# One activation table set behind the tanh, root inputs straight from PSUM, low parts ahead of sums, a last store in three parts

## The reference, cut to what matters

```
def rmsnorm(x, g):
    xf = x.astype(jnp.float32)
    xf = xf * lax.rsqrt(jnp.mean(xf * xf, axis=-1, keepdims=True) + RMS_EPS)
    return (xf * g.astype(jnp.float32)).astype(x.dtype)

def merge_and_mlp(h, gates, y_a, y_b, y_c, w_out, norm_mlp_g, w_up, w_down):
    mixed = gates[0] * y_a + gates[1] * y_b + gates[2] * y_c
    h = h + mixed @ w_out
    hn = rmsnorm(h, norm_mlp_g)
    return h + jnp.square(jax.nn.relu(hn @ w_up)) @ w_down

y_prompt = rmsnorm(h_p, norm_final_g)
y_sample = rmsnorm(h_s, norm_final_g)
```

## Time and profile before

| | before |
|---|---|
| median of 3 runs | 1104.13 us (1103.65 to 1106.02) |
| profiled execution, its own time | 1104.08 us |
| its span, first to last instruction | 1102.3 us |
| PE busy | 1050.9 us (95%) |
| DVE, ACT, POOL busy | 453.5, 422.0, 310.7 us |
| mean granted PE clock | 0.986 of full |

### The profile page before, as it was taken

The page is one execution under the profiler, slowest core; times in us unless marked ns, Lnnn a source line. Parts: engine busy times, 40 slices in busy tenths (PEclk is TensorE's granted clock), DMA queues, the critical chain, the costliest instruction groups (busy, mean ns, idle before and its releaser), DMA issues.

```text
span 1102.3 us, 21957 instructions
## 1 busy us (share of the span) xinstructions
PE 1050.9 (95%) x8694; PEld 947.8 (86%) x8694; DVE 453.5 (41%) x805; ACT 422.0 (38%) x730; POOL 310.7 (28%) x141
## 2 busy tenths in 40 slices
PE   6999999998999989999999999989999999999995
PEld 6886778876778667778999999989999999999995
DVE  5313455775145523333543476743113212212434
ACT  5214556674233222334333323454134224313534
POOL 2422232211222220001212122224443444334620
PEclk9999999999999998999999999999999999999998
DMA  7588887774885575511422325736557367467202
GB/s 270 181 271 300 288 249 232 262 238 153 291 279 197 174 267 178 187 58 40 174 96 88 100 82 190 283 111 248 207 203 272 137 243 284 145 258 267 77 1 78
DMA packets 65945, 211.08 MB, mean 191 GB/s; under 512 B 7850, under 2 KB 10155, under 8 KB 63667
## 3 DMA queue, kind: packets, MB, share of 16 engines
q1 hardware_dynamic: 65842, 209.67, 55.2%
HBM read 202.16 MB, written 51.48 MB: 230 GB/s over the span
## 4 chain that ended last, share of the span: by engine, by line
PE 83%; DVE 5%; ACT 4%; issue 3%; DMA 2%; SPq 1%; POOL 1%; DVEq 0%; ACTq 0%
PE G L1284 52%; PE S L1284 14%; PE Z L1284 11%; PE TR L1287 3%; PE OU L1284 2%; DMA wraw<-in_w_in_dram 2%; ACT whi L681 1%; POOL wlo L653 1%; DVE convy L958 1%; SPq L543 1%; SPq L544 1%; ACT lg L824 0%; DVE mtmp L958 0%; DVE macc L955 0%; DVE pw L1149 0%
## 5 line engine op out<-in xcount | busy, mean ns | idle before, releaser
L1284 PE MATMUL G<-xh,whi 128*128 128x260 f32 x1288 | 380.3, 295 | 14.2 <-DVE xl L958 9.8
L1284 PE MATMUL G<-xl,whi 128*128 128x260 f32 x1288 | 366.8, 285 | 0.0
L1284 PE MATMUL G<-xh,wlo 128*128 128x260 f32 x1288 | 366.1, 284 | 0.0
L653 POOL TENSOR_TENSOR wlo<-wraw,whi 128x1024 fp32r<-128x1024 f32 x61 | 149.1, 2444 | 533.1 <-ACT whi L681 533.1
L1284 PEld LDWEIGHTS G<-xh,whi 128*128 128x128 f32 x1288 | 246.0, 191 | 44.2 <-issue 29.5
L1284 PEld LDWEIGHTS G<-xl,whi 128*128 128x128 f32 x1288 | 245.9, 191 | 0.0
L1284 PEld LDWEIGHTS G<-xh,wlo 128*128 128x128 f32 x1288 | 245.4, 191 | 0.0
L653 POOL TENSOR_TENSOR wlo<-mraw,whi 128x1024 fp32r<-128x1024 f32 x56 | 135.2, 2415 | 201.6 <-ACT whi L681 201.5
L681 ACT ACTIVATE whi<-wraw 128x1024 fp32r<-128x1024 f32 x83 | 87.9, 1059 | 221.8 <-PE G L1284 185.1
L681 ACT ACTIVATE whi<-mraw 128x1024 fp32r<-128x1024 f32 x56 | 59.4, 1061 | 157.3 <-PE G L1284 54.9
L955 DVE TENSOR_TENSOR tg<-G,rstd 128x260 f32<-128x260 f32 x48 | 20.4, 427 | 85.1 <-PE G L1284 85.0
(11 more groups left out here) (261 smaller groups left out, 2090.3 us busy)
## 6 DMA issues: line engine op xcount, KB each, us to landing
wraw<-in_w_in_dram SPq DMA_DIRECT2D x66, 512.0 KB, 5.0
kv<-in_kpool_dram SPq DMA_DIRECT2D x128, 256.0 KB, 3.3
kv<-in_vpool_dram SPq DMA_DIRECT2D x128, 256.0 KB, 3.4
mraw<-in_w_up_dram SPq DMA_DIRECT2D x32, 512.0 KB, 3.5
mraw<-in_w_down_dram SPq DMA_DIRECT2D x32, 512.0 KB, 3.5
out_win_k_kept_dram<-in_cache_win_k_dram SPq DMA_DIRECT2D x8, 2047.0 KB, 9.1
out_win_v_kept_dram<-in_cache_win_v_dram SPq DMA_DIRECT2D x8, 2047.0 KB, 10.5
wraw<-in_w_ab_dram SPq DMA_DIRECT2D x8, 512.0 KB, 3.4
```

What stands on the lines that cost most here:

```text
L653: nc.gpsimd.tensor_tensor(low(u), raw(u)[0], high(u).bitcast(F32), ALU.subtract).then_inc(w_lo, 1)
L1284: return nc.tensor.matmul(out, lhsT, rhs, start=start, stop=stop, **kw)
```

## The change

Four things change.

1. ACT loads the set that has both Ln and Exp once, right behind the last tanh. The eight loads at the second and third norm go.
2. At all three norms Ln reads the bank itself (scale 1/D, bias EPS from a new column of the constants), and DVE makes its variance only after Ln has read the bank (it waits for `xln_made`, `hln_made`, `yln_made`).
3. In the output projection's tiles ACT copies to `xh` ahead of the square, and DVE writes `xl` ahead of the sum (`h_low` ahead of `h_sum`). Besides, ACT writes the high part of the MLP's third unit (`SPLIT_AFTER[UP_TICK + 1]`) at `UP_TICK` itself, ahead of the first tick's squares.
4. At the end the eighth square of each half isn't added on DVE: PE adds it in PSUM with a second matmul. The second half's multiplications and stores come in three parts (3, 3 and 2 tiles).

```diff
+Y_PARTS = (((0, 4), (4, 4)), ((0, 3), (3, 3), (6, 2)))
...
+            def rough_root(out, total, ln_made, root_made, h):
+                nc.scalar.activation(out, total[:, 0:HALF], ACT.Ln, scale=1.0 / D, bias=eps).then_inc(ln_made, 1)
+                act.wait_ge(ln_made, h + 1)
+                nc.scalar.activation(out, out, ACT.Exp, scale=-0.5).then_inc(root_made, 1)
...
-                await_taken(act, "x_var", h)
-                nc.scalar.activation(rstd[:, half(h)], xvar[:, 0, half(h)], ACT.Ln).then_inc(xln_made, 1)
-                act.wait_ge(xln_made, h + 1)
-                nc.scalar.activation(rstd[:, half(h)], rstd[:, half(h)], ACT.Exp, scale=-0.5).then_inc(xroot_made, 1)
+                src = await_bank(act, "x_var", h)
+                rough_root(rstd[:, half(h)], src, xln_made, xroot_made, h)
...
             def h_ready_tile(t):
                 act.wait_ge(dve_took, at("out", t) + 1)
+                act.wait_ge(hn_made, t + 1)
+                copy(xh[:, t, :], hn[:, t % 2, :]).then_inc(hn_hi, 1)
                 if t:
                     act.wait_ge(hacc_made, t)
                 nc.scalar.activation(h2[:], hT[:, t, :], ACT.Square).then_inc(h2_made, 1)
-                act.wait_ge(hn_made, t + 1)
-                copy(xh[:, t, :], hn[:, t % 2, :]).then_inc(hn_hi, 1)
...
-                for v in SPLIT_AFTER.get(k, []):
-                    split_hi(v)
+                if k != UP_TICK + 1:
+                    for v in SPLIT_AFTER.get(k, []):
+                        split_hi(v)
+                if k == UP_TICK:
+                    for v in SPLIT_AFTER.get(k + 1, []):
+                        split_hi(v)
                 if job[0] in ("g0", "g1", "g2"):
                     gate(k, int(job[0][1]), tile, h)
+                    if job[0] == "g2" and tile == KC - 1 and h:
+                        nc.scalar.preload_act_table_set("natural_log_exp_and_others")
...
                 src = await_bank(dve, "x_var", h)
+                dve.wait_ge(xln_made, h + 1)
...
-                    dve.wait_ge(hsum_made, h + 1)
+                    dve.wait_ge(hln_made, h + 1)
...
             def y_sum(n):
+                if n % KC == KC - 1:
+                    return
...
+            def h_low(t):
                 dve.wait_ge(hn_hi, t + 1)
                 tt(xl[:, t, :], hn[:, t % 2, :], xh[:, t, :].bitcast(F32), ALU.subtract).then_inc(hn_lo, 1)
...
                     if tile:
+                        h_low(tile - 1)
                         h_sum(tile - 1)
                     if tile == KC - 1:
+                        h_low(tile)
                         h_sum(tile)
...
             def y_total(h):
+                out = bank[("TR", "OU")[h]][:, 0:HALF]
                 pe.wait_ge(hvar_made, h + 1)
-                pe.wait_ge(yacc_made, KC * (h + 1))
-                mm(bank[("TR", "OU")[h]][:, 0:HALF], ones[:], yacc[:, half(h)], True, True).then_inc(ysum_made, 1)
+                pe.wait_ge(yacc_made, (KC - 1) * (h + 1))
+                mm(out, ones[:], yacc[:, half(h)], True, False)
+                pe.wait_ge(ysq_made, KC * (h + 1))
+                mm(out, ones[:], ysq[:, (KC - 1) % 2], False, True).then_inc(ysum_made, 1)
```

More of the change, by code:

```diff
@@ L296 @@
 for _name, _w in (("gmix", KC), ("gmlp", KC), ("gfin", KC), ("bgate", 3 * KC), ("convw", 12), ("bsb", SBH), ("bcol", 1),
-                  ("st", 64), ("dmask", 8), ("smask", 8), ("sel4", 4), ("sel8", 8)):
+                  ("st", 64), ("dmask", 8), ("smask", 8), ("sel4", 4), ("sel8", 8), ("eps", 1)):
     CV[_name] = (_n, _w)
@@ L351, in decoder_step @@
         dmask, sel4, sel8 = vec("dmask"), vec("sel4"), vec("sel8")
-        smask = vec("smask")
+        smask, eps = vec("smask"), vec("eps")
         xraw = place("xraw", [P, KC, TOK], R + 12928)
@@ L619, in _ @@
                     sp.dma_start(o["conv_old"], x["state_conv"][0, :, 1]).then_inc(conv_copy, 16)
-            for n in range(4):
+            y_parts = [(h, t, w_) for h in range(2) for t, w_ in Y_PARTS[h]]
+            for n, (h, t, w_) in enumerate(y_parts):
                 sp.wait_ge(y_made, n + 1)
-                t = 4 * (n % 2)
-                sp.dma_start(o["y"][:, t:t + 4, half(n // 2)], yT[:, t:t + 4, half(n // 2)]).then_inc(y_out, 16)
-            sp.wait_ge(y_out, 16 * 4)
+                sp.dma_start(o["y"][:, t:t + w_, half(h)], yT[:, t:t + w_, half(h)]).then_inc(y_out, 16)
+            sp.wait_ge(y_out, 16 * len(y_parts))
             sp.wait_ge(win_out, 16 * 6 * NB)
@@ L889, in mlp_root @@
                 for h in range(2):
[L890 to L893, removed]
+                    act.wait_ge(hsum_made, h + 1)
+                    rough_root(rstdb[:, half(h)], bank[("TR", "OU")[h]], hln_made, hroot_made, h)
             def hidden(k, t, h):
@@ L906, in y_square @@
                 act.wait_ge(dve_took, k + 1)
-                if n >= 2:
-                    act.wait_ge(yacc_made, n - 1)
+                if n == KC + 1:
+                    act.wait_ge(ysum_made, 1)
+                elif n >= 2:
+                    act.wait_ge(yacc_made, n - 1 - (n - 2) // KC)
                 nc.scalar.activation(ysq[:, n % 2], hT[:, t, half(h)], ACT.Square).then_inc(ysq_made, 1)
@@ L912, in y_root @@
             def y_root(h):
[L913 to L916, removed]
+                act.wait_ge(ysum_made, h + 1)
+                rough_root(yrstd[:, half(h)], bank[("TR", "OU")[h]], yln_made, yroot_made, h)
             for k, (u, job, h, last) in enumerate(TICKS):
@@ L1111, in y_sum @@
                 else:
-                    dve.wait_ge(yacc_made, n)
+                    dve.wait_ge(yacc_made, n - n // KC)
                     tt(part, part, ysq[:, n % 2], ALU.add).then_inc(yacc_made, 1)
             def y_root(h):
-                dve.wait_ge(ysum_made, h + 1)
+                dve.wait_ge(yln_made, h + 1)
                 nc.vector.tensor_scalar(yvar[:, 0, half(h)], bank[("TR", "OU")[h]][:, 0:HALF], 1.0 / D, EPS, ALU.mult,
@@ L1120, in y_root @@
                 link(polish(yrstd[:, half(h)], yvar[:, 0, half(h)], yvar[:, 1, half(h)]))
[L1121 to L1124, removed]
+                for t, w_ in Y_PARTS[h]:
+                    dve.wait_ge(yg_made, KC * h + t + w_)
+                    part = yT[:, t:t + w_, half(h)]
+                    tt(part, part, yrstd[:, half(h)].unsqueeze(1).to_broadcast([P, w_, HALF]),
                        ALU.mult).then_inc(y_made, 1)
@@ L1646, in column_vectors @@
     put("sel4", ((r // 32)[:, None] == np.arange(4)[None, :]).astype(np.float32))
+    put("eps", EPS)
     put("sel8", ((r % 32 // 4)[:, None] == np.arange(8)[None, :]).astype(np.float32))
```

## The result

| | before | changed |
|---|---|---|
| median, first comparison | 1103.98 us (1103.30 to 1108.82, 6 runs) | 1096.47 us (1094.93 to 1098.62, 6 runs) |
| ratio of the times | | 0.9932, 95% interval 0.9908 to 0.9956 |
| all executions, mean | 1103.74 us (66) | 1097.37 us (12) |
| profiled execution, its own time | 1104.08 us | 1096.90 us |
| its span | 1102.3 us | 1095.1 us |

The change is faster, by 7.5 us in the first comparison and by 6.4 us between the means of all executions of this study (by their scatter 5.4 to 7.4 with 95%).

A forecast was written before the change was run, and what follows sets the result against it. PE was taken to bound the kernel (83% of a 1102.3 us span). Terms 0.3 - 0.35 - 2.9 + 0.44 - 2.1 = -4.6 us, from 1104.08 us, gave 1099.5 us; range 1097.6 to 1101.5.

The forecast's parts named there:

- The low parts at the last output tile: Last output tile: low parts ahead of sums let PE start its eighth block earlier; -0.35 us, bounds 0.28 and 0.62.
- the third unit's high part and the loads: MLP's fifth tick: PE's whole 2.78 us stall for POOL goes, with a restart of 0.1; -2.9 us.
- The end: Last norm and stores: +0.44 us for a second matmul between ticks, -2.1 us from a shorter chain and earlier stores.
- The new load, the other tiles: Load behind the last tanh and the other output tiles: both fit in ACT's idle time; 0 us.
- The first norm: First norm: later second variance and Newton instructions held by POOL lengthen PE's wait; +0.3 us, between +0.1 and +0.6.
- the marks that would have shown the prediction wrong: Wait at MLP's fifth tick or later, over 1.5 us at first norm, last-store gap, or low clock where it was 1.00.
- the rival on a hidden wait: At the end: a table load carries a hidden wait that goes with it, 1.38 us, giving 1098.0; chance 0.02.
- one more: Clock falls once more, or for longer, since ticks stand elsewhere in time: 1.5 us lost, 1101.0; chance 0.14.
- the clock stays up in the MLP's first ticks: MLP's first ticks: the clock no longer falls to 0.50, so 1.5 us come back, 1098.0; chance 0.15.

The follow-up runs named there:

- the kernel with both halves undone: Changed kernel with the second norm's four table loads back and the MLP third unit's high part late again; 1101.35 us, ratio 0.9977.

## Why the prediction missed

**The terms held.** *The low parts at the last output tile* and *the third unit's high part and the loads* were -0.35 and -2.9 and came to -3.27 where the clock did the same in both executions (the order by itself 0.29, between the bounds 0.28 and 0.62). *The end* was +0.44 and -2.1 and came to +0.41 and -2.10. *The new load, the other tiles* was 0: no new wait of PE shows there. *The first norm* was +0.3 and is 0.30 at its place. The sum without the first norm was -4.9, and the four stretches sum to -4.96. Of the marks that would have shown the prediction wrong, only the last one came: low clock in a window that had 1.00, at 10 to 20 us.

A load costs what the rows said. From Ln's start to the Newton step there are now 0.96 us; before it was 2.19 from the earlier trace rows, of which the load is 1.30 (Ln got 0.08 longer). No 1.38 of drain came back on top: the rival on a hidden wait falls, and with it, for this kernel, the figure of the Trainium skill, "ScalarE: Activation LUTs", section "What ACT_TABLE_LOAD costs".

**The step that failed is *The third unit's high part and the loads*, with the clock behind the stall put at nothing.** The term was the wait of 2.78 and "a restart of 0.1", since the one profile at hand showed the clock up behind that wait, and the sum was then made against that one execution. Falls were priced only as rivals, with chances of 0.14 for one more and 0.15 for one less, and the place for one less in the MLP's first ticks. The profiles show falls at five or six places, and they are drawn anew in each execution, but for those near 375 and 413, which all fourteen profiles have. Ahead of the last matmul:

| kernel | where it fell (us) | falls |
|---|---|---|
| before, three profiles (one with the new first norm) | 85, 249, 375, 413 (2), 716; 83, 374, 411 (2), 715, 729 (2); 87, 251, 377, 415 (2), 719 | 6, 7, 6 |
| changed, two profiles | 14, 373, 410 (2), 714; 246, 373, 410 (2), 714 | 5, 5 |
| with the wait of 2.60 cut to 0.43, one profile | 247, 374, 411 (2) | 4 |

At 1.4 us for each, the spans less these falls are 1093.9 and 1093.7 before, 1088.1 and 1088.1 after: 5.6 to 5.8 us. The four stretches behind the last `hn` are 5.0 of it. (The third, with the new first norm, gives 1096.2; there PE's second sum of the first norm was 1.5 us late already, ahead of the edit.) The rest lies ahead of `hn`, within what the wait for weights near 84 us alone varies, 0.80 to 3.33 us in the fourteen profiles.

The rest of the 7.5 us of the first comparison is clock, part of it luck and part the change's own. Luck is about 1.1 us: the means of all executions are 6.4 apart. The change's own part is this: a wait is also a place where the clock can fall. Behind the third unit's stall it fell double in two of the four profiles that have the stall (the second of the kernel before, and the kernel with both halves undone) and in none of the ten without it. Half of the 2.75 us that a double fall cost there is 1.4 us on average beside the 2.8 of the wait, with a wide error from four profiles. The means leave the same: 6.4 - 5.0 = 1.4, give or take 1.0 (1.7, if the first norm's loss of 0.3 reaches the end). The five other kernels without the stall whose stretches, a fall aside, lie within 0.3 us of the changed one's (the first norm back, the high part late, the sums first, the end back, the loads back early) bear it out: their 30 executions take 1097.6 on average, 6.2 below the kernel before (5.4 to 7.0 with 95%).

The rival *the clock stays up in the MLP's first ticks* looked at the wrong place: PE's idle time there stayed about as long (2.60 against 2.34 and 0.59), and the fall at 714 stayed in both profiles of the changed kernel. It isn't certain in the new form, though: behind the one wait of 2.60 it fell in four of seven profiles, behind the two in four of four, behind the one of 0.43 in none of three. Nor are the falls of one execution independent: the three of the seven without one there are the three in which the fall near 413 was single, and in all other profiles that one was double.

So the mechanism, "the whole stall goes, and with it a restart of 0.1", was right, and the size was short: -2.9 was about -4.3 on average, since the restart is 0.1 only when the clock stays up. The prediction had read from one profile that it stays up behind 2.78 us of idling, and took a draw for a rule. The Trainium skill, "TensorE: Matmul & The Clock Gate", section "What's actually happening", says that the chip's window of observation doesn't reset when a kernel starts; that would make falls differ between executions of one program, and the profiles of both kernels agree.

The range of ±2 us was too narrow for the same reason. Executions of the kernel before go from 1098.3 to 1108.8 us, and in the 60 of the experiments their time goes with their mean granted clock: those with 0.985 took 1105.5 on average (10), with 0.986 1104.0 (25), with 0.988 1102.1 (9), with 0.992 1100.4 (3). The three runs known then, 2.4 us apart, showed a part of that spread. The second six of the changed kernel, with a median of 1097.55, lie at the range's edge; the first six missed it by 1.1, which is the luck. Two small slips in the prediction's sums change nothing: the terms' bounds give 1100.1 at the top and not 1100.3, and 1.38 us more at the end would give 1098.1 and not 1098.0.

**What stays open.** Whether the change moves the odds of a fall at 83 to 90 or at 246 to 253, where all kernels have the same code: near 85 it fell in all three profiles of the kernel before (one with the new first norm) and in five of the eleven others, near 249 in two of the three and in seven of the eleven, and luck suffices for both. How likely a double fall behind the third unit's stall is, beyond two of four. And what the first norm's 0.3 us is worth in the end.

## What to carry to other kernels

Price a wait of PE at its length plus the chance of a fall of the clock behind it times what a fall costs in the kernel's own windows; one profile shows a draw, so look at the clock behind the same wait in several. When a change is compared by segments between events of both kernels, terms of 0.3 us can be verified that no median of a kernel with a spread of several us will show. And when two things each remove a stall alone, only undoing both shows what it was worth: the early high part or the missing loads would have done.

## What the runs showed of the hardware

- A fall of the clock lasted 3.41 us at 0.50, or twice that, at every place ahead of the last matmul in all fourteen profiles; it cost 1.4 us (2.75 a double one), not 1.7, since PE's matmuls started 0.217 us apart at half clock and 0.12 at full. Waits of 2.6 to 3.0 us were followed by none, one or two.
- A DVE sum with two SBUF inputs of 128x520 took 2.86 us beside a subtraction of POOL and 0.69 without it. A DVE instruction with one of its inputs in PSUM wasn't held: the sixteen `hT<-hT,G` of 128x260 that started within such a subtraction took 0.42 to 0.43. Moving POOL's start 2.7 us back behind the last `hn` was worth 2.17 us of PE's wait, and with the fall behind it 3.54, while the return of the four loads at this norm alone cost nothing in PE's stretch (36.58 against 36.59).
- A matmul of full float32 by the ones, 128x260, cost PE 0.44 us at full clock (two records of 0.38 us that start 0.22 apart), where the split ones cost 0.12.
